# Up-projection in Strassen's block form: seven half products in place of eight for 20 of 22 column pairs

## The chip, the cores and the metric

The kernel runs on one core of one Trainium2 chip. The metric is the device time of one execution in microseconds (us), the median of several runs. A core has five engines with queues of their own: TensorE (PE; its weight loads are listed as PEld), VectorE (DVE), ScalarE (ACT), GpSimd (POOL) and SyncE (SP, which here only issues transfers). They meet through semaphores.

## The reference

Two layers of a diffusion backbone run over 640 tokens (128 of a prompt, 512 of a grid) with a width of 1024. Each layer has a mixer (retention heads and neighbourhood attention between an input and an output projection) and then the part that is changed here, a gated feed-forward network with a depthwise convolution over three tokens:

```python
D_MODEL, SEQ, DEC_SEQ, D_FF, CONV_W = 1024, 128, 512, 2816, 3
def _conv_ffn(h, w_up, conv_w, conv_b, w_down):
    T = h.shape[1]
    u = h @ w_up
    pad = CONV_W // 2
    up = jnp.pad(u, ((0, 0), (pad, pad), (0, 0)))
    u = sum(up[:, i:i + T] * conv_w[i] for i in range(CONV_W)) + conv_b
    a, gate = jnp.split(u, 2, axis=-1)
    return (jax.nn.silu(gate) * a) @ w_down
```

Prompt and grid are convolved separately. `w_up` is 1024 x 5632, so `u` has 44 columns of 128 channels: 22 value columns and 22 gate columns, which form 22 pairs.

## The kernel before

Channels lie on the 128 partitions and tokens along the free dimension in the up-projection. Every matrix product is made of three matmuls: each operand is split into a high part (written by ScalarE in the fp32r format) and a low part (VectorE: the source minus the high part), and low*high, high*low and high*high are added up in PSUM.

**Up-projection.** The normed and modulated input `aT_hi`, `aT_lo` has 8 blocks of 128 input channels by 640 tokens. For a column `c` `up_product` runs over the 8 blocks `k` and, for the three parts, over two stretches of 384 and 256 tokens in the banks `c` and `c + 4`: 48 matmuls for a column, 96 for a pair. The first four columns are computed as the input becomes ready: first the 384 tokens of all four, then the 256 tokens. The other 40 columns of a layer follow in a loop of 10 rounds with four columns each.

**Round the product.** A column's weights (128 x 1024) arrive from HBM in `raw` slot `c`, by SP's queue in the order of the stream. ScalarE writes `w_hi`, VectorE `w_lo`, which frees the `raw` slot. ScalarE's `column_mid` multiplies the PSUM result by the middle tap into `cv`, VectorE's `column_conv` adds the left tap (three instructions: prompt, grid up to token 384, the rest) and the right tap (three more). For a gate column ScalarE then applies Silu, and VectorE's `gated` multiplies value and gate into `m`. GpSimd does nothing in this part.

**Down-projection.** `m` is split in the same way, and the loop over `w_down` begins in the banks 0, 4, 1, 5, 2 as soon as the last columns have been read.

The order on each engine is the order in which the code is written; there is no scheduler. Semaphores count: `conv_done` (a column's banks are free), `raw_free` (low weights are ready), `w_used`, `hi_done`, `tap_mid`, `silu_done`, `m_done`.

## Time and profile before

| | |
|---|---|
| median of 3 runs | 1676.3 us (1676.21 to 1677.41) |
| span of the profiled execution, first to last instruction | 1674.3 us |
| what the median lies above that span | 2.0 us |
| TensorE busy | 1642.2 us, 98% |
| VectorE / ScalarE / GpSimd busy | 1095.5 / 738.2 / 97.0 us |
| up-projection of the first layer, from the 256-token halves of the first four columns on | 400.1 to 693.3 us |

The profiled execution's own time is not listed beside its span; the 2.0 us are taken to lie around the span in it as well. Busy time of TensorE is modelled from the starts of the matmuls, so its rate is read from the distance between starts.

### The profile page before, as it was taken

To read this page: it belongs to the slowest core of one execution; us is meant where nothing else is said; L and a number is where in the kernel's file an instruction comes from. 1 tells how busy PE (TensorE), PEld (TensorE's weight loads), DVE (VectorE), ACT (ScalarE), POOL (GpSimd) and SP (SyncE) were. 2 spreads that over 40 slices of the span, in tenths; PEclk is the share of its full clock that TensorE was granted. 3 is DMA by queue.
4 is the path that set the end of the run, shared out by engine and by line. 5 is a ranking of instruction groups with operands and counts; after the bars stand their busy time and mean duration, and the time that the engine had idled before them with its cause. 6 is when DMAs were issued, how large, how long until landed. Compare 5 with 4: busy or idle time off the path is not lost.

```text
span 1674.3 us, 26812 instructions
## 1 busy us (share of the span) xinstructions
PE 1642.2 (98%) x10168; PEld 1451.4 (87%) x10168; DVE 1095.5 (65%) x1981; ACT 738.2 (44%) x1273; POOL 97.0 (6%) x86
## 2 busy tenths in 40 slices
PE   8999998999999999999999999999999999999998
PEld 6787896779999999988878889867899999998886
DVE  7866597766555555766678467887665555557575
ACT  6432226556444444433373324373754444443333
POOL 0040060000000000000000400600000000000000
PEclk9999999999999999999999999999999999999999
DMA  9333364433222222344414425727232222224351
GB/s 370 126 124 95 114 217 140 123 102 108 83 74 75 75 75 75 103 157 143 145 38 139 133 64 182 233 77 164 64 101 75 75 75 75 75 75 131 126 171 63
DMA packets 64626, 195.01 MB, mean 116 GB/s; under 512 B 15265, under 2 KB 16673, under 8 KB 64033
## 3 DMA queue, kind: packets, MB, share of 16 engines
q1 hardware_dynamic: 50114, 175.54, 33.4%
q10 hardware_dynamic: 14432, 18.39, 3.3%
q8 instruction: 53, 0.87, 0.2%
q14 instruction: 27, 0.22, 0.0%
HBM read 187.05 MB, written 6.85 MB: 116 GB/s over the span
## 4 chain that ended last, share of the span: by engine, by line
PE 84%; DVE 6%; ACT 3%; issue 2%; DMA 1%; ACTq 1%; SPq 0%; DVEq 0%
PE bank L1737 13%; PE bank L1739 13%; PE bank L1738 13%; PE bank L2074 12%; PE bank L2076 12%; PE bank L2078 12%; DMA raw<-in_stream 1%; DVE ada_sq L1124 1%; PE bank L2014 1%; ACT sp L999 1%; PE bank L1759 1%; DVE w_lo L1113 1%; PE bank L2001 1%; ACTq L711 1%; PE bank L1898 1%
## 5 line engine op out<-in xcount | busy, mean ns | idle before, releaser
L2074 PE MATMUL bank<-aT_hi,w_lo 128*128 128x384 f32 (+1 forms) x1408 | 334.1, 311 | 2.6 <-DVE aT_lo L1164 2.6
L2076 PE MATMUL bank<-aT_lo,w_hi 128*128 128x384 f32 (+1 forms) x1408 | 330.6, 309 | 0.0
L2078 PE MATMUL bank<-aT_hi,w_hi 128*128 128x384 f32 (+1 forms) x1408 | 329.6, 308 | 0.0
L624 ACT ACTIVATE w_hi<-raw 128x1024 fp32r<-128x1024 f32 (+1 forms) x120 | 123.2, 1029 | 400.6 <-PE bank L1739 334.1
L1673 DVE SCALAR_TENSOR_TENSOR cv<-bank,par,cv 128x127 f32<-128x127 f32 (+2 forms) x264 | 99.6, 433 | 252.0 <-ACT cv L1056 252.0
L1113 DVE TENSOR_TENSOR w_lo<-raw,w_hi 128x1024 fp32r<-128x1024 f32 (+1 forms) x120 | 146.2, 1224 | 178.4 <-ACT w_hi L624 178.0
L1737 PE MATMUL bank<-w_hi,aT_lo 128*128 128x512 f32 x560 | 227.3, 406 | 2.2 <-DVE aT_lo L1537 1.9
L2074 PEld LDWEIGHTS bank<-aT_hi,w_lo 128*128 128x128 f32 x1408 | 222.1, 190 | 3.6 <-issue 3.4
L1739 PE MATMUL bank<-w_hi,aT_hi 128*128 128x512 f32 x560 | 222.4, 397 | 0.0
L1738 PE MATMUL bank<-w_lo,aT_hi 128*128 128x512 f32 x560 | 222.2, 397 | 0.0
L2078 PEld LDWEIGHTS bank<-aT_hi,w_hi 128*128 128x128 f32 x1408 | 219.3, 187 | 0.0
L2076 PEld LDWEIGHTS bank<-aT_lo,w_hi 128*128 128x128 f32 x1408 | 219.0, 188 | 0.0
L1055 ACT ACTIVATE cv<-bank,par 128x384 f32<-128x384 f32 x88 | 59.1, 672 | 236.2 <-PE bank L2078 236.0
L1737 PE MATMUL bank<-w_hi,m_lo 128*128 128x512 f32 x400 | 158.7, 397 | 0.0
L1739 PE MATMUL bank<-w_hi,m_hi 128*128 128x512 f32 x400 | 158.6, 396 | 0.0
L1738 PE MATMUL bank<-w_lo,m_hi 128*128 128x512 f32 x400 | 158.6, 396 | 0.0
L1737 PEld LDWEIGHTS bank<-w_hi,aT_lo 128*128 128x128 f32 x560 | 105.8, 189 | 29.4 <-DVE aT_lo L1537 3.4
L1739 PEld LDWEIGHTS bank<-w_hi,aT_hi 128*128 128x128 f32 x560 | 105.7, 189 | 25.7
L1738 PEld LDWEIGHTS bank<-w_lo,aT_hi 128*128 128x128 f32 x560 | 106.0, 189 | 23.3
L1678 DVE SCALAR_TENSOR_TENSOR cv<-bank,par,cv 128x127 f32<-128x127 f32 (+2 forms) x264 | 99.6, 433 | 11.9 <-DVE cv L1673 1.5
L1684 DVE TENSOR_TENSOR w_lo<-raw,w_hi 128x1024 fp32r<-128x1024 f32 x88 | 106.9, 1215 | 0.0
L1061 ACT ACTIVATE w_hi<-raw 128x1024 fp32r<-128x1024 f32 x88 | 92.9, 1055 | 0.0
(213 smaller groups left out, 2365.0 us busy)
## 6 DMA issues: line engine op xcount, KB each, us to landing
raw<-in_stream SPq DMA_DIRECT2D x304, 512.0 KB, 3.7
lead<-in_lead SPq DMA_DIRECT2D x16, 512.0 KB, 10.4
bias<-in_bias ACTq DMA_DIRECT2D x8, 896.0 KB, 10.2
na_v<-vn ACTq DMA_DIRECT2D x2, 1280.0 KB, 5.7
x<-in_xs SPq DMA_DIRECT2D x4, 512.0 KB, 12.1
vt<-na_v ACTq DMA_DIRECT2D x16, 128.0 KB
gb_mix<-gates ACTq DMA_DIRECT2D x2, 1024.0 KB, 5.6
gb_ffn<-gates ACTq DMA_DIRECT2D x2, 1024.0 KB, 4.7
```

Of the source, the lines that this page charges most:

```text
L624: act.activation(w_hi[:, g % 4, 0:n], raw[:, s % 4, 0:n], ACT.Copy).then_inc(hi_done, 1)
L1061: act.activation(w_hi[:, c, :], raw[:, c, :], ACT.Copy).then_inc(hi_done, 1)
L1113: dve.tensor_tensor(w_lo[:, g % 4, 0:n], raw[:, s % 4, 0:n], w_hi[:, g % 4, 0:n].bitcast(F32), ALU.subtract).then_inc(raw_free[s % 4], 1)
L1673: dve.scalar_tensor_tensor(t_[:, lo + 1:lo + 1 + n], ps_[:, off:off + n], tap(0, c, j, layer), t_[:, lo + 1:lo + 1 + n], ALU.mult, ALU.add ...
L1678: i_ = dve.scalar_tensor_tensor(t_[:, lo - 1:lo - 1 + n], ps_[:, off:off + n], tap(2, c, j, layer), t_[:, lo - 1:lo - 1 + n], ALU.mult, AL ...
L1684: dve.tensor_tensor(w_lo[:, c, :], raw[:, c, :], w_hi[:, c, :].bitcast(F32), ALU.subtract).then_inc(raw_free[c], 1)
L1737: pe.matmul(out, ll, rh, start=start, stop=False)
L1738: pe.matmul(out, lh, rl, start=False, stop=False)
L1739: return pe.matmul(out, lh, rh, start=False, stop=stop)
L2074: pe.matmul(out, wl, aT_hi[:, k, tok], start=k == 0, stop=False)
L2076: pe.matmul(out, wh, aT_lo[:, k, tok], start=False, stop=False)
L2078: i_ = pe.matmul(out, wh, aT_hi[:, k, tok], start=False, stop=k == KD - 1)
```

## The change

Only the first four columns (two pairs) of each layer are still computed directly. For each of the other 20 pairs the product is seen as a 2 x 2 block matrix (value column and gate column; lower and upper 512 input channels) times a 2 x 2 block matrix (lower and upper input channels; two halves of the tokens), which takes eight block products directly and seven in Strassen's form (Winograd's variant). A block product is 4 blocks of channels x 3 parts = 12 matmuls of 322 tokens, so a pair has 84 matmuls in place of 96.

- **Tokens.** Two columns of zeros stand behind the prompt and two behind the grid (`GAP`): 644 tokens in two halves of 322 (`HZ`). The zeros between prompt and grid let the convolution run across: `column_conv` has four instructions in place of six. The direct columns use 386 and 256 tokens, the key and query projections 258 and 384.
- **Sums of inputs, once a layer.** Four sums of input blocks (128 x 1288 each): three by VectorE, one by GpSimd (`s_sum`), each split by ScalarE (`s_high`) and VectorE (`s_low`). For this the modulated input is kept whole in `h_all`.
- **Sums of weights, for each pair.** GpSimd forms four sums of 128 x 512 (`first_sum` to `fourth_sum`). Each of the seven weight blocks is split by ScalarE (`block_high`) and VectorE (`block_low`): 7 x 512 elements in place of 2 x 1024.
- **Sums of results, for each pair.** ScalarE copies the first product to `u1` (`keep_first`); VectorE has seven additions of 322 elements, four of which write into a PSUM bank (`first_with_sixth`, `with_seventh`, `gate_late`, `gate_sum`, `value_early`, `value_late`, `gate_early`).
- **`gated`** moves from VectorE to GpSimd. The loops now take two pairs in a round, one in the banks 0, 4, 1, 5 and one in 2, 6, 3, 7; nine rounds on VectorE, ScalarE and GpSimd (the rest is written out ahead and behind), ten on TensorE.
- Buffers are laid out anew; the gains of the feed-forward part (`gb_ffn`) are loaded in two halves, and the split of the first down-weights is written out behind the loop (`down_weight`). In the normalization ahead of the up-projection ScalarE's `modulate` no longer waits for a buffer of two tiles. The weights that are streamed, their number and their order in SP's queue are the same.

```diff
+        def spare(e):
+            return (t2_even, t2_odd)[e][:]
...
+        def block_source(n, e):
+            a_, g_ = raw[:, 2 * e, :], raw[:, 2 * e + 1, :]
+            return (a_[:, 0:W], spare(e), a_[:, 0:W], g_[:, 0:W], a_[:, W:2 * W], spare(e), g_[:, W:2 * W])[n]
...
+        def block_of(w_, n):
+            return w_[:, n // 2, n % 2 * W:(n % 2 + 1) * W]
...
+                def first_sum(i, e):
+                    pool.wait_ge(*pair_full(2 * e, i, layer))
+                    pool.wait_ge(*pair_full(2 * e + 1, i, layer))
+                    a_, g_ = raw[:, 2 * e, 0:W], raw[:, 2 * e + 1, 0:W]
+                    pool.tensor_tensor(g_, g_, a_, ALU.subtract).then_inc(t1_done, 1)
+                def second_sum(i, e):
+                    pool.wait_ge(t1_done, at(t1_done, layer, nth(i, e) + 1))
+                    pool.tensor_tensor(spare(e), raw[:, 2 * e + 1, W:2 * W], raw[:, 2 * e + 1, 0:W],
+                                       ALU.subtract).then_inc(t2_done, 1)
+                def third_sum(i, e):
+                    pool.wait_ge(blk_lo, at(blk_lo, layer, 5 * nth(i, e) + 2))
+                    pool.wait_ge(t2_done, at(t2_done, layer, nth(i, e) + 1))
+                    a_ = raw[:, 2 * e, 0:W]
+                    pool.tensor_tensor(a_, spare(e), a_, ALU.subtract).then_inc(t3_done, 1)
+                def fourth_sum(i, e):
+                    pool.wait_ge(t3_done, at(t3_done, layer, nth(i, e) + 1))
+                    pool.tensor_tensor(spare(e), spare(e), raw[:, 2 * e, W:2 * W], ALU.subtract).then_inc(t4_done, 1)
+                def gated(i, e):
+                    q = pair_of(i, e)
+                    pool.wait_ge(silu_done, at(silu_done, layer, q + 1))
+                    t_ = m[:, bass.ds(q, 1), :]
+                    pool.tensor_tensor(t_, t_, cvg[:, e:e + 1, :], ALU.mult).then_inc(m_done, 1)
...
+                pool.wait_ge(s_sum_done, at(s_sum_done, layer, 3))
+                pool.wait_ge(s_lo_done, at(s_lo_done, layer, 1))
+                pool.tensor_tensor(s_sum[:, 0], h_part(0, 1), s_sum[:, 1], ALU.subtract).then_inc(s_sum_done, 1)
+                third_sum(1, 0)
+                fourth_sum(1, 0)
+                gated(None, 0)
+                pool.wait_ge(w_used, at(w_used, layer, W_UP0 + G_ONE))
+                second_sum(1, 1)
+                third_sum(1, 1)
+                fourth_sum(1, 1)
+                gated(None, 1)
+                with pool.Fori(1, NSP // 2) as i:
+                    for e in range(2):
+                        pool.wait_ge(c_sum, at(c_sum, layer, 5 * nth(i, e) + 5))
+                        first_sum(i + 1, e)
+                        second_sum(i + 1, e)
+                        third_sum(i + 1, e)
+                        fourth_sum(i + 1, e)
+                        gated(i, e)
+                gated(NSP // 2, 0)
+                gated(NSP // 2, 1)
...
+                def block_high(n, i, e, first=False):
+                    if n in (0, 4):
+                        act.wait_ge(*pair_full(2 * e, i, layer))
+                    elif n == 6:
+                        act.wait_ge(*pair_full(2 * e + 1, i, layer))
+                    else:
+                        done = {1: t2_done, 2: t3_done, 3: t1_done, 5: t4_done}[n]
+                        act.wait_ge(done, at(done, layer, nth(i, e) + 1))
+                    if first:
+                        act.wait_ge(w_used, at(w_used, layer, W_UP0 + n // 2 + 1))
+                    else:
+                        act.wait_ge(blk_mm, at(blk_mm, layer, PROD * nth(i, e) + (n + 1 - PROD)))
+                    act.activation(block_of(w_hi, n), block_source(n, e), ACT.Copy).then_inc(blk_hi, 1)
...
+                def keep_first(i, e):
+                    act.wait_ge(blk_mm, at(blk_mm, layer, PROD * nth(i, e) + 1))
+                    act.wait_ge(c11_done, at(c11_done, layer, nth(i, e)))
+                    act.activation(u1[:], bank[UP_BANKS[e][0]][:, 0:HZ], ACT.Copy).then_inc(u1_done, 1)
...
+                def block_low(n, i, e):
+                    dve.wait_ge(blk_hi, at(blk_hi, layer, PROD * nth(i, e) + n + 1))
+                    i_ = dve.tensor_tensor(block_of(w_lo, n), block_source(n, e), block_of(w_hi, n).bitcast(F32), ALU.subtract)
+                    if n == 5:
+                        i_.then_inc(raw_free[2 * e], 1)
+                    elif n == 6:
+                        i_.then_inc(raw_free[2 * e + 1], 1)
+                    else:
+                        i_.then_inc(blk_lo, 1)
...
+                def first_with_sixth(i, e):
+                    dve.wait_ge(u1_done, at(u1_done, layer, nth(i, e) + 1))
+                    dve.wait_ge(blk_mm, at(blk_mm, layer, PROD * nth(i, e) + 2))
+                    dve.tensor_tensor(u2[:], bank[UP_BANKS[e][1]][:, 0:HZ], u1[:], ALU.add).then_inc(c_sum, 1)
...
+                def gate_sum(i, e):
+                    dve.wait_ge(c_sum, at(c_sum, layer, 5 * nth(i, e) + 3))
+                    dve.tensor_tensor(u2[:], bank[UP_BANKS[e][3]][:, 0:HZ], u2[:], ALU.add).then_inc(u4_done, 1)
...
-                with dve.Fori(0, KF // 2 - 1) as j:
-                    for c in range(4):
-                        column_conv(j, c)
-                        column_weight(j, c)
-                        if c >= 2:
-                            gated(j, c - 2)
...
+                dve.wait_ge(norm_lo, at(norm_lo, layer, 2 * NT))
+                dve.tensor_tensor(s_sum[:, 0], h_part(1, 0), h_part(1, 1), ALU.add).then_inc(s_sum_done, 1)
+                dve.wait_ge(s_sum_done, at(s_sum_done, layer, 1))
+                dve.tensor_tensor(s_sum[:, 1], s_sum[:, 0], h_part(0, 0), ALU.subtract).then_inc(s_sum_done, 1)
+                dve.tensor_tensor(s_sum[:, 2], h_part(0, 0), h_part(1, 0), ALU.subtract).then_inc(s_sum_done, 1)
+                column_conv(None, 0, 0)
+                block_low(0, 1, 0)
+                block_low(1, 1, 0)
+                s_low(0)
+                s_low(1)
+                column_conv(None, 0, 1)
+                block_low(2, 1, 0)
+                block_low(3, 1, 0)
+                s_low(2)
+                block_low(4, 1, 0)
+                block_low(5, 1, 0)
+                column_conv(None, 1, 0)
+                block_low(6, 1, 0)
+                s_low(3)
...
+                with dve.Fori(1, NSP // 2) as i:
+                    for e in range(2):
+                        gate_early(i, e)
+                        column_conv(i, e, 0)
+                        block_low(6, *after(i, e))
+                        block_low(0, i + 1, e)
+                        block_low(1, i + 1, e)
+                        first_with_sixth(*after(i, e))
+                        column_conv(i, e, 1)
+                        with_seventh(*after(i, e))
+                        gate_late(*after(i, e))
+                        gate_sum(*after(i, e))
+                        for n in range(2, 4):
+                            block_low(n, i + 1, e)
+                        value_early(*after(i, e))
+                        block_low(4, i + 1, e)
+                        value_late(*after(i, e))
+                        block_low(5, i + 1, e)
...
-                with pe.Fori(1, KF // 2) as j:
-                    for c in range(4):
-                        pe.wait_ge(raw_free[c], at(raw_free[c], layer, j + (S_UP0 // 4 + 1)))
-                        pe.wait_ge(conv_done, at(conv_done, layer, 4 * j + c - 3))
-                        for k in range(KD):
-                            up_product(c, (0, 1), k, True)
+                def block_product(n, e, lhs, rhs_hi, rhs_lo):
+                    out = bank[UP_BANKS[e][lhs]][:, 0:HZ]
+                    for k in range(HP):
+                        wh, wl = (block_of(w_, n)[:, k * P:(k + 1) * P] for w_ in (w_hi, w_lo))
+                        pe.matmul(out, wl, rhs_hi[:, k, :], start=k == 0, stop=False)
+                        pe.matmul(out, wh, rhs_lo[:, k, :], start=False, stop=False)
+                        i_ = pe.matmul(out, wh, rhs_hi[:, k, :], start=False, stop=k == HP - 1)
+                    i_.then_inc(blk_mm, 1)
...
+                with pe.Fori(1, KF // 2) as i:
+                    for e in range(2):
+                        low_ready(0, i, e)
+                        pe.wait_ge(conv_done, at(conv_done, layer, 2 * nth(i, e) + 1))
+                        block_product(0, e, 0, *a_part(0, 0))
+                        low_ready(1, i, e)
+                        block_product(1, e, 1, s2_hl[:, 0], s2_hl[:, 1])
+                        low_ready(2, i, e)
+                        pe.wait_ge(conv_done, at(conv_done, layer, 2 * nth(i, e) + 2))
+                        block_product(2, e, 2, s31_hi[:, 0], s31_lo[:, 0])
+                        low_ready(3, i, e)
+                        block_product(3, e, 3, s31_hi[:, 1], s31_lo[:, 1])
+                        low_ready(4, i, e)
+                        pe.wait_ge(u1_done, at(u1_done, layer, nth(i, e) + 1))
+                        block_product(4, e, 0, *a_part(0, 1))
+                        pe.wait_ge(*pair_freed(2 * e, i, layer))
+                        pe.wait_ge(c_sum, at(c_sum, layer, 5 * nth(i, e) + 1))
+                        block_product(5, e, 1, *a_part(1, 1))
+                        pe.wait_ge(*pair_freed(2 * e + 1, i, layer))
+                        pe.wait_ge(c_sum, at(c_sum, layer, 5 * nth(i, e) + 3))
+                        pe.wait_ge(u4_done, at(u4_done, layer, nth(i, e) + 1))
+                        pe.wait_ge(s_lo_done, at(s_lo_done, layer, 4))
+                        block_product(6, e, 3, *a_part(1, 0))
```

VectorE in the loop, before: one gate column and the product that follows it (two such columns make a pair).

```order
L1673 SCALAR_TENSOR_TENSOR cv<-bank0,par,cv 128x127
L1673 SCALAR_TENSOR_TENSOR cv<-bank0,par,cv 128x256
L1673 SCALAR_TENSOR_TENSOR cv<-bank4,par,cv 128x255
...
L1678 SCALAR_TENSOR_TENSOR cv<-bank0,par,cv 128x127
L1678 SCALAR_TENSOR_TENSOR cv<-bank0,par,cv 128x255
L1678 SCALAR_TENSOR_TENSOR cv<-bank4,par,cv 128x256
...
L1684 TENSOR_TENSOR w_lo<-raw,w_hi 128x1024 [waits hi_done]
...
L1689 TENSOR_TENSOR m<-cv 128x640
```

VectorE in the loop, now: the first 12 of the 22 computing steps of one pair (`t2_even` is a sum of weights, `u1` to `u3` are partial results).

```order
L1983 TENSOR_TENSOR bank5<-bank5,u2 128x322 [waits u4_done]
...
L1925 SCALAR_TENSOR_TENSOR m<-bank0,par,m 128x322
...
L1925 SCALAR_TENSOR_TENSOR m<-bank4,par,m 128x319
...
L1928 SCALAR_TENSOR_TENSOR m<-bank0,par,m 128x321
...
L1931 SCALAR_TENSOR_TENSOR m<-bank4,par,m 128x320
...
L1942 TENSOR_TENSOR w_lo<-raw,w_hi 128x512 [waits blk_hi]
...
L1942 TENSOR_TENSOR w_lo<-raw,w_hi 128x512 [waits blk_hi]
...
L1942 TENSOR_TENSOR w_lo<-t2_even,w_hi 128x512 [waits blk_hi]
...
L1953 TENSOR_TENSOR u2<-bank6,u1 128x322 [waits blk_mm]
...
L1958 TENSOR_TENSOR u3<-bank3,u2 128x322 [waits c_sum]
...
L1963 TENSOR_TENSOR bank3<-bank7,u3 128x322 [waits c_sum]
...
L1967 TENSOR_TENSOR u2<-bank7,u2 128x322 [waits c_sum]
```

The `gated` product is gone from VectorE, and between the taps of one pair now stand weight blocks of the next but one pair and sums of results of the next pair; the 22 are 8 taps, 7 weight blocks and 7 sums of results.

TensorE in the loop, before: the beginning of a column.

```order
L2199 ISA [waits raw_free0]
L2074 MATMUL bank0<-aT_hi,w_lo 128x384 [waits conv_done]
L2074 MATMUL bank4<-aT_hi,w_lo 128x256
L2076 MATMUL bank0<-aT_lo,w_hi 128x384
L2076 MATMUL bank4<-aT_lo,w_hi 128x256
L2078 MATMUL bank0<-aT_hi,w_hi 128x384
L2078 MATMUL bank4<-aT_hi,w_hi 128x256
```

TensorE in the loop, now: the first matmuls of the seven products of a pair, with what each waits for.

```order
L2570 ISA [waits blk_lo]
L2554 MATMUL bank0<-aT_hi,w_lo 128x322 [waits conv_done]
L2555 MATMUL bank0<-aT_lo,w_hi 128x322
L2556 MATMUL bank0<-aT_hi,w_hi 128x322
...
L2554 MATMUL bank4<-s2_hl,w_lo 128x322 [waits blk_lo]
L2555 MATMUL bank4<-s2_hl,w_hi 128x322
...
L2554 MATMUL bank1<-s31_hi,w_lo 128x322 [waits conv_done]
...
L2554 MATMUL bank5<-s31_hi,w_lo 128x322 [waits blk_lo]
...
L2554 MATMUL bank0<-aT_hi,w_lo 128x322 [waits u1_done]
...
L2554 MATMUL bank4<-aT_hi,w_lo 128x322 [waits c_sum,raw_free0]
...
L2554 MATMUL bank5<-aT_hi,w_lo 128x322 [waits u4_done,s_lo_done,c_sum,raw_free1]
```

A column waited for its weights and for its banks; each product now waits for its own weight block, and the last three wait besides for sums of results that VectorE makes from the first four.

VectorE where the up-projection begins, now, from the last part of the normalization on (in the kernel before the taps of the first column stood here directly).

```order
L1990 TENSOR_TENSOR s_sum<-h_all 128x1288 [waits norm_lo]
L1992 TENSOR_TENSOR s_sum<-s_sum,h_all 128x1288 [waits s_sum_done]
L1993 TENSOR_TENSOR s_sum<-h_all 128x1288
L1925 SCALAR_TENSOR_TENSOR m<-bank0,par,m 128x386 [waits tap_mid]
...
L1942 TENSOR_TENSOR w_lo<-raw,w_hi 128x512 [waits blk_hi]
L1942 TENSOR_TENSOR w_lo<-t2_even,w_hi 128x512 [waits blk_hi]
L1938 TENSOR_TENSOR s31_lo<-s_sum,s31_hi 128x1288 [waits s_hi_done]
L1938 TENSOR_TENSOR s2_hl<-s_sum,s2_hl 128x1288 [waits s_hi_done]
L1925 SCALAR_TENSOR_TENSOR cvg<-bank1,par,cvg 128x386 [waits tap_mid]
...
L1942 TENSOR_TENSOR w_lo<-raw,w_hi 128x512 [waits blk_hi] x2
L1938 TENSOR_TENSOR s31_lo<-s_sum,s31_hi 128x1288 [waits s_hi_done]
```

GpSimd at the same place; it had no instruction here before.

```order
L652 TENSOR_TENSOR raw<-raw 128x512 [waits raw_full1,raw_full0]
L656 TENSOR_TENSOR t2_even<-raw 128x512 [waits t1_done]
L652 TENSOR_TENSOR raw<-raw 128x512 [waits raw_full3,raw_full2]
L683 TENSOR_TENSOR s_sum<-h_all,s_sum 128x1288 [waits s_lo_done,s_sum_done]
L663 TENSOR_TENSOR raw<-t2_even,raw 128x512 [waits t2_done,blk_lo]
L667 TENSOR_TENSOR t2_even<-t2_even,raw 128x512 [waits t3_done]
L673 TENSOR_TENSOR m<-m,cvg 128x642 [waits silu_done]
```

TensorE's loop waits for `s_lo` of three sums (the third is the last row of VectorE), and ahead of that stand weight blocks which rest on GpSimd's third sum of weights, behind GpSimd's sum of inputs.

## Rows read from the trace of the kernel before

**Rows 1.** The page, its head and its busy line of TensorE: us, share, instructions.
```profile
span 1674.3 us, 26812 instructions
...
PE 1642.2 (98%) x10168; PEld 1451.4 (87%) x10168; DVE 1095.5 (65%) x1981; ACT 738.2 (44%) x1273; POOL 97.0 (6%) x86
```

**Rows 2.** What TensorE waited for, whole run: us in total, times, longest.
```profile
PE bank L2074 <- DVE aT_lo L1164: 2.6, 2, 1.3
PE bank L2085 <- DMA cond_row<-in_cond: 2.6, 1, 2.6
```

**Rows 3.** Windows of the first layer: length, then busy us of each engine, PEclk.
```profile
400.11:411.70 11.59, 11.59 (x98) 11.59 (x98) 5.40 (x13) 7.82 (x11) 0.00 (x0) 1.00 0.20 62
411.70:693.26 281.56, 281.56 (x1923) 281.56 (x1921) 157.29 (x312) 123.57 (x162) 0.00 (x0) 1.00 0.25 79
424.00:494.35 70.35, 70.35 (x482) 70.35 (x481) 39.21 (x80) 30.88 (x40) 0.00 (x0) 1.00 0.23 75
```

**Rows 4.** Timeline of TensorE, 384-wide and later 256-wide matmuls: start, duration.
```profile
396.23 0.34 PE L2078 MATMUL bank<-aT_hi,w_hi 128*128 128x384 f32 x1
...
397.99 0.34 PE L2074 MATMUL bank<-aT_hi,w_lo 128*128 128x384 f32 x1
...
404.82 0.28 PE L2074 MATMUL bank<-aT_hi,w_lo 128*128 128x256 f32 x1
...
407.94 0.28 PE L2078 MATMUL bank<-aT_hi,w_hi 128*128 128x256 f32 x1
```

**Rows 5.** Groups of VectorE by line and shape: busy us, mean ns of one.
```profile
L1684 DVE TENSOR_TENSOR w_lo<-raw,w_hi 128x1024 fp32r<-128x1024 f32 x88 | 106.9, 1215 | 0.0
...
L1673 DVE SCALAR_TENSOR_TENSOR cv<-bank,par,cv 128x256 f32<-128x256 f32 x88 | 41.9, 476 | 0.0
...
L1241 DVE TENSOR_TENSOR t<-bank,rope 128x256 f32<-128x256 f32 x32 | 11.9, 414 | 0.0
...
L1480 DVE TENSOR_TENSOR y_ffn<-bank,gb_ffn 128x512 f32<-128x512 f32 x10 | 6.1, 679 | 0.0
...
L1113 DVE TENSOR_TENSOR w_lo<-raw,w_hi 128x512 fp32r<-128x512 f32 x8 | 5.5, 692 | 29.1 <-ACT w_hi L624 29.1
```

**Rows 6.** Timeline of VectorE in the loop, one column: start, duration.
```profile
483.67 1.13 DVE L1673 SCALAR_TENSOR_TENSOR cv<-bank,par,cv 128x127 f32<-128x127 f32 x3 [2.14 <-ACT cv L1056]
484.94 1.13 DVE L1678 SCALAR_TENSOR_TENSOR cv<-bank,par,cv 128x127 f32<-128x127 f32 x3
485.99 1.22 DVE L1684 TENSOR_TENSOR w_lo<-raw,w_hi 128x1024 fp32r<-128x1024 f32 x1
```

**Rows 7.** Groups of ScalarE by line and shape: busy us, mean ns of one.
```profile
L1061 ACT ACTIVATE w_hi<-raw 128x1024 fp32r<-128x1024 f32 x88 | 92.9, 1055 | 0.0
L1055 ACT ACTIVATE cv<-bank,par 128x384 f32<-128x384 f32 x88 | 59.1, 672 | 236.2 <-PE bank L2078 236.0
L1056 ACT ACTIVATE cv<-bank,par 128x256 f32<-128x256 f32 x88 | 49.1, 558 | 0.0
...
L624 ACT ACTIVATE w_hi<-raw 128x512 fp32r<-128x512 f32 x8 | 5.1, 632 | 41.5 <-PE bank L1739 41.5
```

**Rows 8.** Timeline of GpSimd, ahead of the attention part: start, duration.
```profile
118.16 6.04 POOL L523 TENSOR_TENSOR tm<-tm,kdec 128x512 f32<-128x512 f32 x5 [6.46 <-PE bank L1824]
124.16 2.39 POOL L539 TENSOR_TENSOR dtab<-dtab,ident 128x1024 f32<-128x1024 f32 x1
```

**Rows 9.** Timeline of VectorE while GpSimd is at work, two places.
```profile
110.93 1.86 DVE L1113 TENSOR_TENSOR w_lo<-raw,w_hi 128x1024 fp32r<-128x1024 f32 x1 [6.33 <-ACT w_hi L624]
...
240.65 1.61 DVE L1113 TENSOR_TENSOR w_lo<-raw,w_hi 128x1024 fp32r<-128x1024 f32 x1
```

**Rows 10.** Timeline where the up-projection's second halves begin: VectorE, then TensorE.
```profile
398.76 1.23 DVE L1164 TENSOR_TENSOR aT_lo<-tf,aT_hi 128x1024 fp32r<-128x1024 f32 x1 [1.32 <-ACT aT_hi L658]
...
400.11 0.32 PE L2074 MATMUL bank<-aT_hi,w_lo 128*128 128x256 f32 x1
```

More of the change, by code:

```diff
@@ L170, in build @@
         raw = sb("raw", [P, SLOTS, 1024])
+        with ExitStack() as s:
+            below = sb("below", [P, SLOTS * 1024 - W], F32, s)
+            t2_odd = sb("t2_odd", [P, W], F32, s)
         w_hi = sb("w_hi", [P, SLOTS, 1024], F32R)
@@ new lines, in _ @@
+                last = NSP // 2
+                gate_early(last, 0)
+                column_conv(last, 0, 0)
+                block_low(6, last, 1)
+                first_with_sixth(last, 1)
+                down_low(0, 0, mx[:, 1, 0], mx[:, 0, 0])
+                column_conv(last, 0, 1)
+                with_seventh(last, 1)
+                split_lo(W_DOWN0, layer)
+                gate_late(last, 1)
+                gate_sum(last, 1)
+                down_low(0, 1, mx[:, 1, 1], mx[:, 0, 1])
```

416 lines of the change are left out of this document (302 added, 114 removed).

## The prediction

> **What bounds the kernel now.** I read the page first: TensorE is busy for 1642.2 of 1674.3 us [rows 1]. The longest single wait of TensorE is 2.6 us, on the first transfer; the one at the up-projection is 1.3 us in each layer, on the low part of the input [rows 2]. The windows then tell the stage apart: in the loop of 40 columns (281.56 us a layer) TensorE has no idle time, in five pairs of it (70.35 us, so 14.07 us a pair) VectorE works 39.2 us and ScalarE 30.9 us, GpSimd nothing, and the granted clock is full [rows 3]. So fewer matmuls give time here until another engine takes TensorE's place. VectorE has 44% to spare, and the change spends just that.
>
> **TensorE's gain.** The distance between starts is 1.76 / 10 = 0.176 us for 384 tokens and 3.12 / 26 = 0.120 us for 256 [rows 4], 0.46 and 0.47 ns a token; the loop gives 281.56 / 960 = 0.293 us for each 640 [rows 3], which is 0.458 ns a token too. A matmul of 322 is then 0.148 us, a product of 12 is 1.776 us, a pair of 84 is 12.43 us. Twenty pairs take 248.6 us where they took 281.6: 33 us less a layer, 66 us in all. That is the most this change can give.
>
> **VectorE in the loop.** Durations come from [rows 5]; back to back an instruction costs some 0.08 us less than it lasts (in [rows 6] the group from 484.94 ends at 486.07 and the next starts at 485.99), and one that waits for its own predecessor loses these 0.08 and 0.14 more (484.80 to 484.94).
> - Seven weight blocks of 512: 0.692 - 0.08 = 0.61 each, 4.3 us.
> - Eight tap instructions of about 321: 0.476 for 256 plus 66 x 1.04 ns (the slope of 414 to 679 ns for 256 to 512) = 0.545, less 0.08 = 0.465; 3.7 us.
> - Seven sums of results of 322 with a PSUM source: 0.414 + 0.07 - 0.08 = 0.40, two of them in a chain (+0.22 each): 3.3 us.
>
> Together 11.3 us in 12.43. Four of the sums write PSUM, for which no row stands; reading PSUM costs nothing beside SBUF (679 against 692 ns), which I take for writing as well, with the 0.14 us of a hand-over [rows 6] for each as the upper end, 0.6 us a pair.
>
> Then GpSimd. It now makes four sums of 512 (6.04 / 5 = 1.21 us each, and 2.39 for 1024 [rows 8]) and the product of 642 (1.5), so it works 6.4 us of each pair. While it works VectorE's subtraction of 1024 took 1.61 and once 1.86 us [rows 9] where it takes 1.22 [rows 6], a third to a half more. Taps and sums of results have one source in SBUF, weight blocks two; I let only the weight blocks pay. About half of them meet GpSimd: 4.3 x 0.5 x 0.32 to 0.52 = 0.7 to 1.1 us. VectorE then needs 12.0 to 12.4 us, and with the PSUM term 13.0: at TensorE's 12.43 or just above it. If all weight blocks met GpSimd at the worst rate it were 11.3 + 2.2 + 0.6 = 14.1 us. I take 12.5 us a pair, since nothing is left over for VectorE's own waits: 250 us a layer, bounds 12.43 and 14.1.
>
> ScalarE has 7 blocks at 0.63, four middle taps and the first copy at about 0.615 (between 0.558 and 0.672), and Silu: under 8.5 us [rows 7]. It isn't the bound. The streamed bytes are the same, and a pair's raw slots are freed two pairs ahead, so transfers stay hidden.
>
> **Entry of the stage, each layer.** This is where I expect most to be lost. The second halves start at 400.11, when the low part of the input ends at 398.76 + 1.23 [rows 10], and last 11.6 us [rows 3]. Counted from there, by the order of the code:
> - VectorE's three sums of 1288 (1.215 + 264 x 1.04 ns = 1.49 each): ended at 4.5. ScalarE splits them (1.055 + 264 x 0.83 ns = 1.27 each, the slope from 632 to 1055 ns): ended at 6.0, then applies the first middle taps: 7.1.
> - VectorE waits for that (from 4.5 to 7.2), then taps 1.9, two weight blocks 1.2, and the low part of the first sum 1.5: 11.9.
> - GpSimd's sum of inputs waits for this one; 2.33 ns an element (from 2.39 us for 1024) makes 3.0 for 1288: 15.0. Its third sum of weights follows: 16.3. ScalarE's block: 17.1. VectorE, with taps and another sum long done, makes blocks 2 and 3: 18.5, and then the third low part: 20.2.
>
> TensorE's loop waits for that third low part, so it stands still from 11.6 to about 20.4: **8.8 us**. Bounds: 7 if GpSimd's 1288 take less than its rate says, 11 if all that has two SBUF sources is slowed by a third.
>
> VectorE enters the loop late, since the taps of the second direct pair, two blocks, the fourth low part and all weight blocks of the next pair stand ahead of `gate_early` of the first pair. By the same counting this one starts at 37.5, where TensorE has ended that pair at 32.8; the sums for the next pair are ready at 46.4, and its last product could begin at 43.4: **3 us** more. Behind that VectorE has little slack to win back time, but needs none.
>
> **Exit.** The first down-tile needs banks of the last but one pair, which are read by then. The second pair of `m` blocks is behind all taps and one weight split: sums and taps of the last pair 0.5 + 2 x 1.9, split 1.1, two blocks 1.5, waits 0.6: 7.5 us after the last product, where five tiles of down-projection take 30 x 512 x 0.458 ns = 7.0. **0.8 us** with its wait. Wider matmuls (386 for 384, 258 for 256): 1152 tokens more in both layers, 0.5 us.
>
> **Sum.** A layer: -281.6 + 250.0 + 8.8 + 3 + 0.8 = -19.0 us. Both: -38.0, with the widths -37.5. From the span 1674.3 that is 1636.8, and with the 2.0 us that the median lies above the span **1639 us**. Measured differences under 0.2% (3.4 us) can't be told from no change.
>
> **Rivals.**
> 1. VectorE is the bound (the upper part of my own range, 12.7 to 13.4 us a pair). For it: 12.0 to 13.0 us of work before any wait. Against: the taps and sums are each placed well behind the product that they wait for. At 13.0: +20 us, 1659.
> 2. The entry is hidden better than I count, and VectorE has slack: a stop of 4 us and no late sums, 12.43 a pair. 1639 - 2 x (4.8 + 3 + 1.4) = 1621. Against: the chain goes through four engines, and each step is in the code.
> 3. TensorE's clock falls in the stop of 8.8 us. No row shows the lower level: the clock is full in all windows, but no wait before was above 2.6 us. At half the clock (1.2 GHz) a product takes 1.78 us longer; two of them a layer are 7 us in all, of which the later 3 us wait hides up to 6. 1640 to 1646.
> 4. **Slower.** GpSimd holds VectorE up for longer than the rows show. The mechanism: `block_low` has both sources in SBUF, as have all of GpSimd's instructions, and the loop can't be faster than VectorE. What is lost outside the loop is 25.7 us, so the gain is gone when a pair takes 14.07 - 25.7 / 40 = 13.43 us, 2.2 us more than VectorE's bare 11.3. At my worst case, 14.1, it is 1676 + 40 x 0.67 = 1703.
> 5. Nothing is gained because the seventh of a product is not a seventh of the time: excluded but for a few per cent, as time follows tokens in all three widths.
>
> The Trainium skill (SBUF — State Buffer, "SBUF: two separate sides") has a harder rule than these rows: VectorE with two SBUF inputs and GpSimd share a read port under an exclusive lock, and the loser blocks for the whole instruction. By that, an estimate: each block that meets one of GpSimd's 1.21 us waits for half of it, 7 x 0.5 x 0.6 = 2.1 us, 13.4 us a pair, which would be 1676, no gain at all. The rows bear it out only in part: VectorE lost 0.39 us per 1024, with GpSimd at work without a break (19 instructions in 25.17 us [rows 9]).
>
> On rival 3 the Trainium skill (TensorE: Matmul & The Clock Gate, "Part 1: The HAM clock gate") says that the clock falls to half when the engine has idled and comes back under work; no row here shows it, as the clock is at its upper level throughout.
>
> **How the numbers follow.** Chances: my forecast 0.44, rival 1 0.26, rival 2 0.11, rival 3 0.10, rival 4 0.06, rival 5 0.03. My own terms give 1632 (entry 7, pair 12.43, no PSUM term) to 1648. The range of 8 in 10 leaves out most of rival 2, rival 4 and the upper end of rival 1: 1629 to 1662. Faster by more than 0.2%: 0.44 + 0.26 + 0.11 + 0.10 = 0.91; the same 0.03; slower 0.06.
>
> **What the profile after would show.** (a) Starts of 322-token matmuls 0.148 us apart; 0.16 would cost 40 us. (b) A stop of TensorE of 7 to 11 us ahead of its loop, released by the low part of a sum of inputs, and a clock below full behind it if rival 3 holds. (c) In the middle of the loop, a pair every 12.4 to 12.6 us with VectorE at 11.5 to 12.4; if it is rival 1 or 4, TensorE waits in each pair for `u2`/bank sums or `w_lo`, and VectorE has no idle time. (d) Weight blocks of 512 at 0.7 to 1.0 us. (e) A wait of about 3 us in the second pair. I would be wrong most where VectorE's instructions on PSUM or next to GpSimd cost more than their nearest rows.

## The result, and the profile after it

The changed kernel takes 1663.7 us in the median (1663.1 to 1664.6, 4 runs) where the kernel before takes 1676.5 (1676.2 to 1677.4): a ratio of 0.9923, 95% interval 0.9909 to 0.9937. It is faster, by 12.8 us. The forecast was 37 us, and the upper end of the range, 1662, is 1.7 us below the median.

The head of its page and the busy line, to be read against [rows 1]:

```profile
span 1662.8 us, 28242 instructions
...
PE 1589.2 (96%) x9688; PEld 1391.8 (84%) x9688; DVE 1316.7 (79%) x2255; ACT 782.2 (47%) x1483; POOL 395.9 (24%) x302
```

TensorE lost 53 us of work and the span only 11.5. The difference is idle time, and the list of what TensorE waited for (us in total, times, longest), against [rows 2], names these waits among the new ones:

```profile
PE bank L2554 <- DVE u L1967: 20.6, 38, 1.4
PE bank L2554 <- DVE s_lo L1938: 17.9, 2, 9.0
...
PE bank L2087 <- DVE m_lo L1987: 3.5, 3, 1.6
```

The second is the stop ahead of the loop, once a layer. The first comes 38 times: nearly every pair waits for VectorE's `gate_sum`. The third is at the exit of the loop. The windows of layer 1, against [rows 3] (length, busy us of PE, PEld, DVE, ACT, POOL, then the granted clock), show the stretch behind the stop, the rest of the loop, and 100 us from its middle:

```profile
420.76:424.00 3.24, 3.24 (x12) 3.24 (x13) 3.24 (x3) 3.24 (x7) 2.75 (x2) 0.50 0.00 0
424.00:687.90 263.90, 252.83 (x1671) 248.04 (x1669) 247.55 (x437) 139.57 (x257) 128.25 (x94) 1.00 0.26 81
550.00:650.00 100.00, 96.08 (x638) 94.26 (x637) 94.57 (x168) 51.66 (x96) 51.47 (x38) 1.00 0.25 79
```

In the middle of the loop TensorE and VectorE are both busy for 95 or 96% and neither for all of it: two engines that hand work to each other. TensorE's timeline (start, duration, and what it waited for) at the entry and in the middle of the loop, against [rows 4]:

```profile
420.76 0.63 PE L2554 MATMUL bank<-aT_hi,w_lo 128*128 128x322 f32 x1 [8.90 <-DVE s_lo L1938]
421.19 0.47 PE L2555 MATMUL bank<-aT_lo,w_hi 128*128 128x322 f32 x1
421.46 0.47 PE L2556 MATMUL bank<-aT_hi,w_hi 128*128 128x322 f32 x1
...
540.40 0.31 PE L2555 MATMUL bank<-aT_lo,w_hi 128*128 128x322 f32 x1
540.55 0.31 PE L2556 MATMUL bank<-aT_hi,w_hi 128*128 128x322 f32 x1
541.26 0.39 PE L2554 MATMUL bank<-aT_hi,w_lo 128*128 128x322 f32 x1 [0.41 <-DVE u L1967]
```

The stop is 8.90 us. Behind it the first 17 matmuls start 0.27 us apart, at a granted clock of 0.50, where they are 0.15 us apart later. The last row is the one stop of a pair, ahead of its seventh product. I took the time between the first matmuls of successive pairs from the same timeline: 14.64 and 15.65 us for the first two, and then 13.09 and 13.26 in turn, 13.17 in the mean. The times of a pair given below are read in the same way.

VectorE's groups of the loop (busy us, mean ns of one), against [rows 5]:

```profile
L1942 DVE TENSOR_TENSOR w_lo<-raw,w_hi 128x512 fp32r<-128x512 f32 x200 | 187.1, 966 | 9.4 <-ACT w_hi L1256 9.4
...
L1942 DVE TENSOR_TENSOR w_lo<-t_odd,w_hi 128x512 fp32r<-128x512 f32 x40 | 27.2, 680 | 0.0
...
L1963 DVE TENSOR_TENSOR bank<-bank,u 128x322 f32<-128x322 f32 x40 | 20.0, 501 | 1.5
```

A weight block takes 0.68 us where nothing disturbs it, and 0.97 in the mean of the 200 others. The sums that read and write PSUM are undisturbed. VectorE's timeline from one `gate_sum` (L1967) to the next pair's taps, and GpSimd's beside it, show where (start, duration):

```profile
540.51 0.49 DVE L1967 TENSOR_TENSOR u<-bank,u 128x322 f32<-128x322 f32 x1
540.92 2.56 DVE L1942 TENSOR_TENSOR w_lo<-raw,w_hi 128x512 fp32r<-128x512 f32 x2
543.41 0.48 DVE L1972 TENSOR_TENSOR bank<-bank,u 128x322 f32<-128x322 f32 x1
...
545.41 0.48 DVE L1983 TENSOR_TENSOR bank<-bank,u 128x322 f32<-128x322 f32 x1
546.64 1.01 DVE L1925 SCALAR_TENSOR_TENSOR m<-bank,par,m 128x322 f32 x2 [0.74 <-ACT m L1234]
...
548.48 1.48 DVE L1942 TENSOR_TENSOR w_lo<-raw,w_hi 128x512 fp32r<-128x512 f32 x2
```

```profile
540.76 1.57 POOL L673 TENSOR_TENSOR m<-m,cvg 128x642 f32 x1 [0.71 <-ACT cvg L1217]
546.14 1.30 POOL L652 TENSOR_TENSOR raw<-raw 128x512 f32<-128x512 f32 x1 [3.80 <-DVE bank L1983]
547.52 1.30 POOL L656 TENSOR_TENSOR t_even<-raw 128x512 f32<-128x512 f32 x1
```

Two blocks that last 1.28 us by themselves take 2.56 where GpSimd's gating product has just begun: 540.76 + 1.57 is 542.33, and two undisturbed blocks from there would end at 543.6; these end at 543.5. At 548.48 GpSimd's second sum has 0.34 us to go, and two blocks lose 0.2. A pair loses 1.3 + 0.15 us in this way, and 0.7 us more in a wait of the taps for ScalarE (546.64). Without both, VectorE's rows of a pair add up to 11.0 us.

At the exit, TensorE, VectorE and GpSimd:

```profile
696.62 0.47 PE L2087 MATMUL bank<-w_hi,m_lo 128*128 128x512 f32 x1 [1.63 <-DVE m_lo L1987]
```

```profile
694.92 1.56 DVE L1987 TENSOR_TENSOR m_lo<-m,m_hi 128x642 fp32r<-128x642 f32 x2
```

```profile
695.85 4.32 POOL L673 TENSOR_TENSOR m<-m,cvg 128x642 f32<-128x642 f32 x1 [9.57 <-ACT cvg L1217]
```

The last gating product takes 4.32 us in place of 1.57, while VectorE runs `m_lo`, a weight block and a custom operation, all with two SBUF sources, without a gap. Here it is GpSimd that is held up. TensorE does not wait for it: the two `m_lo` blocks that release TensorE end at 696.48, and this product ends at 700.17.

### The profile page after: what moved, and what is told of

It reads as the page before. It is cut to its first block, busy times and chain, and to the rows that moved or that the text cites. A ratio compares the mean times of both kernels' runs of the same rounds, so it can differ in the third digit from the quotient of the medians.

```text
span 1662.8 us, 28242 instructions
## 1 busy us (share of the span) xinstructions
PE 1589.2 (96%) x9688; PEld 1391.8 (84%) x9688; DVE 1316.7 (79%) x2255; ACT 782.2 (47%) x1483; POOL 395.9 (24%) x302
## 4 chain that ended last, share of the span: by engine, by line
PE 54%; DVE 23%; issue 10%; ACT 6%; DVEq 1%; ACTq 1%; DMA 1%; POOL 1%; SPq 0%; POOLq 0%
PE bank L2087 13%; PE bank L2088 12%; PE bank L2089 12%; DVE w_lo L1942 3%; PE bank L2554 3%; PE bank L2556 3%; PE bank L2555 3%; DVE cvg L1925 1%; ACT m L1234 1%; DVE w_lo L1358 1%; DVE cvg L1931 1%; DVE m L1931 1%; DVE bank L1963 1%; DVE u L1967 1%; DVE u L1953 1%
## 5 line engine op out<-in xcount | busy, mean ns | idle before, releaser
L2554 PE MATMUL bank<-aT_hi,w_lo 128*128 128x322 f32 x640 | 203.5, 318 | 40.4 <-DVE u L1967 20.6
L2555 PE MATMUL bank<-aT_lo,w_hi 128*128 128x322 f32 x640 | 200.1, 313 | 0.0
L2556 PE MATMUL bank<-aT_hi,w_hi 128*128 128x322 f32 x640 | 199.3, 311 | 0.0
L1942 DVE TENSOR_TENSOR w_lo<-raw,w_hi 128x512 fp32r<-128x512 f32 x200 | 187.1, 966 | 9.4 <-ACT w_hi L1256 9.4
L1256 ACT ACTIVATE w_hi<-raw 128x512 fp32r<-128x512 f32 x200 | 121.0, 625 | 112.3 <-POOL raw L663 112.3
L2554 PEld LDWEIGHTS bank<-aT_hi,w_lo 128*128 128x128 f32 x640 | 121.2, 189 | 50.4 <-issue 49.4
L2555 PEld LDWEIGHTS bank<-aT_lo,w_hi 128*128 128x128 f32 x640 | 122.0, 191 | 0.0
L2556 PEld LDWEIGHTS bank<-aT_hi,w_hi 128*128 128x128 f32 x640 | 121.9, 191 | 0.0
L642 POOL TENSOR_TENSOR bias<-bias,masks 128x192 f32<-128x192 f32 (+1 forms) x48 | 59.0, 1267 | 199.4 <-DMA bias<-in_bias 199.4
L2556 PE MATMUL bank<-s_hi,w_hi 128*128 128x322 f32 x320 | 99.8, 312 | 0.0
```

The lines of the kernel that those rows point to most:

```text
L642: i_ = pool.tensor_tensor(part, part, masks[:, m0 * CG:(m0 + n) * CG].rearrange("p (g c) -> p g c", c=CG).unsqueeze(2) .to_broadcast([P, n ...
L1256: act.activation(block_of(w_hi, n), block_source(n, e), ACT.Copy).then_inc(blk_hi, 1)
L1942: i_ = dve.tensor_tensor(block_of(w_lo, n), block_source(n, e), block_of(w_hi, n).bitcast(F32), ALU.subtract)
L2554: pe.matmul(out, wl, rhs_hi[:, k, :], start=k == 0, stop=False)
L2555: pe.matmul(out, wh, rhs_lo[:, k, :], start=False, stop=False)
L2556: i_ = pe.matmul(out, wh, rhs_hi[:, k, :], start=False, stop=k == HP - 1)
```

## The experiments

Each version ran on the same chip as a run of the kernel before (1676.1 to 1676.7 us there). Ratios are to it, with their 95% interval.

**1. Half of GpSimd's work gone.** Three theories stood at the start. A: VectorE sets the pace, with its blocks waiting out GpSimd's instructions and with the wait for ScalarE. B: VectorE is slowed in proportion to GpSimd's busy time. C: the ring of product, ScalarE's copy and VectorE's sum sets the pace. The four weight sums of a pair in the loop are cut to 8 of 512 columns (this part of the computation is left out).

```
-                        first_sum(i + 1, e)
+                        first_sum(i + 1, e, 8)      # and the three others
```

> GpSimd's four sums of weights in the loop are cut to 8 of 512 elements (so most of each sum is left out); its product value x gate stays whole. Theory A: in the loop VectorE is the bound at 13.17 us a pair, of which 1.45 us is lost by weight blocks that wait out a GpSimd instruction to its end, and almost all of that (1.3) on the one product, because two weight blocks stand right where it runs. The sums cost 0.15 to 0.3 us only: 12.9 us a pair, 1653 to 1659. Theory B: VectorE is slowed in proportion to GpSimd's busy time (6.8 us a pair, 5.2 of it sums): 1.1 us of the 1.45 go, TensorE is the bound again at 12.43, 1632 to 1638. Theory C: not VectorE's time but the ring product, ScalarE, VectorE, product sets the pace: no change, 1664.

1651.7 us, 0.9853 (0.9837 to 0.9870). Just below A's range, far from B's and C's. A pair takes 12.77 us (12.89 in the second layer); its blocks beside the gating product still wait, 1.0 us in place of 1.3, since the product now starts 0.41 us ahead of them and not 0.16. VectorE, and then GpSimd:

```profile
549.62 2.30 DVE L1942 TENSOR_TENSOR w_lo<-raw,w_hi 128x512 fp32r<-128x512 f32 x2
```

```profile
549.21 1.56 POOL L673 TENSOR_TENSOR m<-m,cvg 128x642 f32 x1 [2.64 <-ACT cvg L1217]
```

GpSimd's busy time in the loop fell from 51 to 18 us in 100, and 1.0 of the 1.45 us of loss stayed (12.77 - 11.0 - 0.7): it is not the busy time, but which instruction meets which.

**2. All of it gone.** The gating product of the loop is cut to 8 of 642 columns as well.

> As before, and the product value x gate in the loop cut to 8 of 642 elements too, so GpSimd is all but idle in the loop (sums and product are left out but for 8 elements). Theories A and B: weight blocks take 0.68 us again, VectorE needs 11.0 us and 0.74 of waiting for ScalarE, below TensorE's 12.43, which becomes the bound: 18 x 2 x 0.74 us less, and about 2 us of the late second pair, 1633 (1630 to 1638). Theory C: 1664 and TensorE still stops ahead of the seventh product.

1637.0 us, 0.9761 (0.9745 to 0.9778). Each pair from the third on takes 12.44 us. The window of 100 us in the loop:

```profile
550.00:650.00 100.00, 100.00 (x678) 100.00 (x677) 90.11 (x178) 59.35 (x106) 12.14 (x40) 1.00 0.28 84
```

TensorE has no idle time; theory C is out, and the sum of seven products, 12.43 us, is right.

**3. The gating product back on VectorE.** Nothing is left out. GpSimd keeps the four sums.

```
-                        gated(i, e)                 # GpSimd, behind fourth_sum
+                        gated(i, e)                 # VectorE, behind gate_sum
```

> The product value x gate goes back to VectorE (0.74 us there), behind the chain of sums; GpSimd keeps the four sums. Theory A: +0.74 and -1.3 a pair, 12.6 us, 20 to 24 us less: 1640 to 1645. Theory B: +0.74 and -0.33, 13.6 us a pair: 1678. Theory C: the chain ahead of the seventh product is not longer, no change: 1664.

1646.7 us, 0.9818 (0.9802 to 0.9835), 1.7 us above A's range and far from that of B, which is out. VectorE gained work and got faster:

```profile
548.88 0.82 DVE L1978 TENSOR_TENSOR m<-m,cvg 128x642 f32 x1
549.62 1.29 DVE L1931 TENSOR_TENSOR w_lo<-raw,w_hi 128x512 fp32r<-128x512 f32 x2
```

It pays 0.74 us and its two blocks get 1.27 back. A pair takes 12.54 and 12.74 us in turn. Against that the stop ahead of the loop is 10.0 us in place of 8.9.

**4. The wait for ScalarE taken away.** `value_late` goes ahead of the fifth block, so that ScalarE's middle tap is ready sooner.

```
-                        block_low(4, i + 1, e)
                         value_late(*after(i, e))
+                        block_low(4, i + 1, e)
```

> In VectorE's loop value_late stands ahead of the fifth weight block, not behind it: the middle taps of ScalarE start 0.6 us earlier, and VectorE's wait for them (0.74 us a pair) shrinks to about 0.15. Nothing is left out. Theory A (VectorE's time is the bound, its own waits included): 12.6 us a pair, 1640 to 1645. Theory C: the first product's banks are free earlier but nothing else moves, 1660 to 1664.

1663.5 us, 0.9921 (0.9905 to 0.9938): nothing gained, and A's figure missed by 19 us. The wait is gone from the rows, and this stands in its place, on VectorE and on GpSimd:

```profile
545.22 1.01 DVE L1925 SCALAR_TENSOR_TENSOR m<-bank,par,m 128x322 f32 x2
...
547.06 2.08 DVE L1942 TENSOR_TENSOR w_lo<-raw,w_hi 128x512 fp32r<-128x512 f32 x2
```

```profile
546.70 1.30 POOL L656 TENSOR_TENSOR t_even<-raw 128x512 f32<-128x512 f32 x1
```

The taps start at once, the blocks behind them are ready 0.7 us sooner against GpSimd's sums (which VectorE's `gate_early` releases, so they move with it), and they wait out 0.8 us of the second sum where they waited 0.2. The window from the middle of the loop has VectorE busy for 158 of 160 us, and no faster:

```profile
500.00:660.00 160.00, 153.65 (x1019) 150.69 (x1018) 157.98 (x267) 85.06 (x159) 82.39 (x61) 1.00 0.26 79
```

A fell in its number, not in its mechanism: what VectorE no longer waits for ScalarE it now waits for GpSimd.

**5. GpSimd's instruction moved, nothing else.** If that holds, the same work in another order must do. `gated` of a pair runs one pair later, right behind the fourth sum, and so 0.67 us earlier against the two blocks that it meets. Nothing is left out.

```
-                        gated(i, e)
+                        gated(i - 1 + e, 1 - e)
```

> One edit of c1_lag alone: GpSimd's gating product of a pair follows the fourth weight sum of the next pair, so that it starts 0.67 us earlier against the two weight blocks that wait for it; VectorE's order is that of the changed kernel. Theory A (exclusive, instruction by instruction): the two blocks wait 0.6 to 0.7 us and not 1.3, the pair falls from 13.17 to 12.5 or 12.6 us, 17 pairs a layer: 1641 to 1645. A theory in which it is the 0.74 us wait for ScalarE that sets the pair: 1660 to 1664.

1638.0 us, 0.9767 (0.9751 to 0.9783): 3 us below A's range, and 26 us less than the changed kernel, from the place of one instruction. VectorE, and GpSimd:

```profile
546.22 1.83 DVE L1942 TENSOR_TENSOR w_lo<-raw,w_hi 128x512 fp32r<-128x512 f32 x2
```

```profile
545.32 1.57 POOL L673 TENSOR_TENSOR m<-m,cvg 128x642 f32 x1
```

The product ends at 546.89, the blocks wait 0.6 us where they waited 1.3, and a pair takes 12.44 us from the third on (12.47 in the second layer): TensorE is the bound. The wait for ScalarE (0.66 us) is still in VectorE's rows, so it did not set the pace by itself.

**6. The blocks moved too.** Both value sums go ahead of blocks 2 to 5, on top of 5.

```
-                        for n in range(2, 4):
-                            block_low(n, i + 1, e)
                         value_early(*after(i, e))
-                        block_low(4, i + 1, e)
                         value_late(*after(i, e))
-                        block_low(5, i + 1, e)
+                        for n in range(2, 6):
+                            block_low(n, i + 1, e)
```

> All of GpSimd's work stays, at the same length, but its gating product is done one pair later, right behind the fourth weight sum (0.7 us earlier than now), and VectorE forms both value sums ahead of the four weight blocks, so that these stand 0.8 us later. Theory A (a block of two SBUF sources that is ready while a GpSimd instruction runs waits for that instruction's end, and nothing else is slowed): the two blocks no longer meet the gating product, the 0.74 us wait for ScalarE is gone as well, and VectorE needs 11.0 + 0.8 us, under TensorE's 12.44 us: 1637 to 1641. Theory D (the loss moves to another pair of instructions, as it did when only the value sum was put ahead, which gave nothing): 1650 to 1664. Theory B (loss in proportion to GpSimd's busy time): 13.17 less 0.74 at best, but 1.45 of contention kept, 1640 to 1664 with blocks lengthened as before.

1635.6 us, 0.9758 (0.9742 to 0.9774), just below A's range. VectorE in one pair:

```profile
546.87 0.50 DVE L1977 TENSOR_TENSOR bank<-u,bank 128x322 f32<-128x322 f32 x1 [0.35 <-PE bank L2554]
547.28 1.89 DVE L1942 TENSOR_TENSOR w_lo<-raw,w_hi 128x512 fp32r<-128x512 f32 x3
...
551.92 2.16 DVE L1942 TENSOR_TENSOR w_lo<-raw,w_hi 128x512 fp32r<-128x512 f32 x2
```

The three blocks at 547.28 are undisturbed (3 x 0.6 + 0.1), those at 551.92 lose 0.9 to GpSimd's second sum, and VectorE now waits for TensorE.

**7. The entry.** TensorE waits for the low halves of the input sums one by one.

```
-                pe.wait_ge(s_lo_done, at(s_lo_done, layer, 3))
...
                         low_ready(1, i, e)
+                        pe.wait_ge(s_lo_done, at(s_lo_done, layer, 2))
...
                         low_ready(2, i, e)
+                        pe.wait_ge(s_lo_done, at(s_lo_done, layer, 3))
```

> One edit at the entry of the loop: TensorE waits for the low halves of the input sums just ahead of the product that reads them, not for all three ahead of the first product. Theory T1: the stop ahead of the first product (8.9 us a layer) is the cost, so starting two products early saves their time, 3.5 us a layer: 1656 to 1658. Theory T2: the first two pairs are paced by the chain on VectorE and GpSimd (blocks, taps, sums of the second pair), which this edit leaves where it is; TensorE starts early and waits longer for the third product and for the second pair: 1661 to 1664.

1664.7 us, 0.9930 (0.9914 to 0.9947): nothing, as theory T2 has it. The loop starts at 410.9 in place of 420.8, and its first two pairs take 22.2 and 17.2 us in place of 14.6 and 15.7. The third pair starts 39.3 us after the last direct matmul, where it was 39.2. The stop was moved, not shortened: when the second pair ends is set by VectorE and GpSimd.

**8. GpSimd's order at the entry.** With 7, the third and fourth weight sums go ahead of the fourth input sum, and `s_low(2)` ahead of blocks 2 and 3.

> The edit of b1, and two more at the entry: GpSimd forms the third and fourth weight sum of the first pair ahead of the fourth input sum (6.0 or 3.8 us), and VectorE forms the third input's low half ahead of the blocks that wait for those sums. T1: 1650 to 1656 (the first three products no longer wait for GpSimd). T2: the chain on VectorE loses its idle 2.62 us ahead of the third block and the wait of TensorE for the third product falls from 9 us to about 5, but the second pair keeps its own late sums: 1654 to 1659. If what GpSimd does first only moves its cost to the seventh product's input: 1661 to 1664.

1664.3 us, 0.9925 (0.9909 to 0.9942): nothing again, against both T1 and T2. VectorE and GpSimd at the entry:

```profile
416.30 6.84 DVE L1942 TENSOR_TENSOR w_lo<-raw,w_hi 128x512 fp32r<-128x512 f32 x3
```

```profile
409.75 3.90 POOL L663 TENSOR_TENSOR raw<-t_even,raw 128x512 f32<-128x512 f32 x1 [12.55 <-DVE w_lo L1942]
...
414.97 3.97 POOL L685 TENSOR_TENSOR s_sum<-h_all,s_sum 128x1288 f32<-128x1288 f32 x1
418.89 2.01 POOL L673 TENSOR_TENSOR m<-m,cvg 128x642 f32<-128x642 f32 x1
420.86 1.74 POOL L656 TENSOR_TENSOR t_odd<-raw 128x512 f32<-128x512 f32 x1
```

GpSimd's sum of 512 takes 3.90 us beside VectorE's two low halves of 1288, and VectorE's three blocks (1.9 us) take 6.84, as each waits out one of GpSimd's. What stands on either side of the entry is the same work in turns, and its order matters little.

**9. 6 and 8 together.**

> The edits of c1_lag and b3_entry together. Theory A with T1: 1624 to 1630. Theory A with T2: 1629 to 1634. Theory D: 1645 or more.

1635.6 us, 0.9758 (0.9741 to 0.9774): as 6 alone, and 1.6 us above the range that T2 gave. The entry edits are worth nothing here either.

**10. The input sum off GpSimd.** 9, with the fourth input sum on VectorE behind `s_low(2)`. Nothing is left out.

```
-                pool.tensor_tensor(s_sum[:, 0], h_part(0, 1), s_sum[:, 1], ALU.subtract).then_inc(s_sum_done, 1)
...
                 s_low(2)
+                dve.tensor_tensor(s_sum[:, 0], h_part(0, 1), s_sum[:, 1], ALU.subtract).then_inc(s_sum_done, 1)
                 block_low(2, 1, 0)
```

> c1_lag, the entry edits of b3_entry, and the fourth input sum (3.8 us on GpSimd) formed by VectorE, ahead of the blocks that wait for it now. Theory T2 (the entry is paced by the turns that VectorE's blocks and GpSimd's long instructions take at each other's cost): VectorE does 1.4 us more and waits 5 us less, its taps for the second pair start about 4 us earlier, and with them the end of the loop: 1627 to 1631. If the entry is paced by something else: 1634 to 1637 as c1_lag and c2_all.

1633.0 us, 0.9740 (0.9723 to 0.9756): 2.6 us less than 9 where 5 to 9 were expected. That is a small gain: 9 ran on another chip, where the kernel before took 0.4 us more, and the two intervals overlap. The traces bear it out, as the first pair takes 20.9 us where it takes 22.1 in 9, in each layer. VectorE's three blocks:

```profile
417.42 4.32 DVE L1939 TENSOR_TENSOR w_lo<-raw,w_hi 128x512 fp32r<-128x512 f32 x3
```

They still meet the gating product and a weight sum. This is the lowest time of all versions: 43 us below the kernel before, 31 below the changed one.

## Why the prediction missed

**The step that failed** is the VectorE term of the loop: "I take 12.5 us a pair, since nothing is left over for VectorE's own waits". It measured 13.17. The 11.3 us of bare work were a little high (11.0). The contention, "about half of them meet GpSimd: 0.7 to 1.1 us", measured 1.4 to 1.5. A hand-over was left out: the taps wait 0.7 us for ScalarE's middle taps, which start 0.4 us after `value_late` (L1977) and last 1.1 us, while VectorE has only a block and a sum to do in between. 11.0 + 1.45 + 0.7 is 13.15. Over 17 pairs a layer 0.67 us make 11.4 us, 23 in all, of the 26 by which the span missed.

**Why the contention was mis-sized**: I took it as a rate, a share of the blocks slowed by a third to a half. The runs show it as an event: a VectorE instruction with two SBUF sources that is ready while one of GpSimd's runs starts when that one ends. A mean over the kernel hides this. The trace of the kernel before had it already, and I misread [rows 9]. These are GpSimd's instructions there, each from a narrow window of the timeline, as a wider one merges them:

```profile
109.31 2.39 POOL L533 TENSOR_TENSOR dtab<-dtab,pr 128x1024 f32<-128x1024 f32 x1
...
239.59 1.58 POOL L546 TENSOR_TENSOR bias<-bias,masks 128x192 f32<-128x192 f32 x1
...
251.36 0.59 POOL L546 TENSOR_TENSOR bias<-bias,masks 128x192 f32<-128x192 f32 x1
```

The 1.61 us at 240.65 stand beside instructions of 192 columns that last 0.59 us while VectorE is idle (251.36) and 1.58 here: each engine waited out the other's instruction in turn, and VectorE lost 0.39 us only because GpSimd's were short. The 1.86 us at 110.93 stand beside the last 0.8 us of the instruction from 109.31. So "the rows bear it out only in part" was wrong: they bear it out, and GpSimd was "at work without a break" only because it was held up as well. The price is set by where each block stands: two meetings a pair, but one of them with GpSimd's longest instruction, at its start. Experiments 3, 5 and 6 move the meeting and get back what it cost; 4 moves it the wrong way; 1 and 2 shorten it. The Trainium skill (SBUF — State Buffer, "SBUF: two separate sides") states this rule, and the rows agree with it in kind (2.56 us for 1.28). The 13.4 us that I had worked out from it rested on my guess that half of the seven blocks wait for half of a GpSimd instruction, 2.1 us in all. They came within 0.25 us of the measured pair by luck: the waits were 1.45 us, in two meetings, and the 0.7 us for ScalarE were not in that sum. It stood there without a chance of its own.

**Rival 1** is what happened: VectorE is the bound, with the wait that it foretold, for `u`. Its price at 13.17 is 1639 + 40 x 0.67 = 1665.8, and the run gave 1663.7. The mechanism of **rival 4**, GpSimd holding VectorE up for longer than I had read from the rows, is what raised the pair that far; it stayed below the 13.43 us at which the gain would be gone. The clock of **rival 3** fell too: after the stop it was 0.50, half of its upper level (1.2 for 2.4 GHz), and the first pair took 14.64 us for 12.44.

**The other terms.** TensorE's gain was right: 0.148 us a matmul, 12.44 a pair. The stop was forecast at 8.8 us and was 8.90, and the chain to it came as counted to within 0.6 us at each step, though GpSimd's sum of 1288 took 3.8 us for 3.0. The second pair was forecast 3 us late and was 15.65 - 12.44 = 3.2, but by luck, as two things moved together. TensorE ended the first pair 35.3 us after 400.1 for 32.8, most of it by the clock, and VectorE reached `gate_early` (L1983) at 40.0 for 37.5. VectorE's blocks ahead of that had met GpSimd's instructions again, where 0.68 us is the bare block:

```profile
420.33 2.04 DVE L1942 TENSOR_TENSOR w_lo<-raw,w_hi 128x512 fp32r<-128x512 f32 x1
422.29 1.76 DVE L1942 TENSOR_TENSOR w_lo<-t_even,w_hi 128x512 fp32r<-128x512 f32 x1
...
434.94 3.81 DVE L1942 TENSOR_TENSOR w_lo<-raw,w_hi 128x512 fp32r<-128x512 f32 x3 [2.07 <-ACT w_hi L1256]
```

The first two pairs together took 2.3 us a layer more than forecast. That the clock cost this is not shown: by experiment 7 it is VectorE and GpSimd that set the end of the second pair, so a faster first pair may only have waited longer in the second. The PSUM term is zero: 0.50 us for a sum that writes PSUM (L1963) beside 0.49 for one that writes SBUF (L1967). The exit cost 2.2 us a layer in place of 0.8, 1.8 in the stop at 694.8 and 0.4 in a later one. VectorE is behind there: the sums behind the last product take 1.3 us where I had counted 0.5, and the wait for ScalarE is 0.8 us, so the `m_lo` blocks end 8.6 us after that product and not 7.5.

**Two gains were not forecast.** Matmuls of the down-projection start closer. These rows are 57 matmuls apart, first after, then before:

```profile
739.82 0.40 PE L2088 MATMUL bank<-w_lo,m_hi 128*128 128x512 f32 x1
...
753.04 0.40 PE L2088 MATMUL bank<-w_lo,m_hi 128*128 128x512 f32 x1
```

```profile
739.63 0.40 PE L1737 MATMUL bank<-w_hi,m_lo 128*128 128x512 f32 x1
...
752.99 0.39 PE L1737 MATMUL bank<-w_hi,m_lo 128*128 128x512 f32 x1
```

13.22 / 57 is 0.232 us, 13.36 / 57 is 0.234. Over all 660 of a layer, without the stops, it is 1.3 us less. The blocks `m_hi` and `m_lo` have other strides and addresses now; which of the two does it, if either, was not tried. And the attention part of layer 2 is 2.3 us shorter, that of layer 1 is not. Its cause is open.

The account of the span, a layer: 17 pairs 11.4, the first two 2.3, the last one 0.5, exit 1.4, stop 0.1, down-projection -1.3, together 14.4. Twice that, less 2.3, is 26.5 us, where the difference is 26.0: forecast 1636.8, measured 1662.8.
